# Transposes of two attention stages split off, and products of the conditioning vectors moved ahead of them

## What is computed

```
sh1, sc1, g1, sh2, sc2, g2 = split(silu(c) @ w_ada[l] + b_ada[l], 6)     # conditioning vectors, also for c_ctx
h  = rmsnorm(x) * (1 + sc1) + sh1                                        # 4 tiles of 128 tokens
q, k, v = projections of h @ w_in                                        # 8 MLA heads and 4 differential heads
p  = softmax(q k^T * scale)           # MLA head: one map.  differential head: p0 - lam * p1, two maps
o  = p v ;  x = x + g1 * (concat(o, rmsnorm(o_diff)) @ w_out)
h  = rmsnorm(x) * (1 + sc2) + sh2
x  = x + g2 * peer_ffn(h)             # 8 heads x 16 picked experts for each token, rows gathered from HBM
```

## Time and profile before

| | us |
|---|---|
| median of 3 runs | 2626.43 (2625.87 to 2627.11) |
| the profiled execution, its own time | 2625.7 |
| its span in the trace | 2623.7 |
| granted TensorE clock, mean | 0.904 |

### The profile page before, as it was taken

One profiled execution on the slowest core, in us unless ns is written; L12 is line 12 of the kernel. 1 busy time (PEld: TensorE's weight loads), 2 busy tenths in 40 slices (PEclk: granted clock), 3 DMA queues, 4 the chain that ended last, 5 costly groups with the idle time before them and its releaser, 6 DMA issues.

```text
span 2623.7 us, 26515 instructions
## 1 busy us (share of the span) xinstructions
PE 2058.3 (78%) x6888; PEld 1072.0 (41%) x6888; DVE 1854.4 (71%) x4488; ACT 1162.2 (44%) x3122; POOL 969.7 (37%) x916
## 2 busy tenths in 40 slices
PE   5997778777988877888777697779777887667765
PEld 2555444543444444444334244334553444333322
DVE  0147986895567879886979766655597786877776
ACT  2123484344237543853434723432244754433333
POOL 1013344342434333543443444420133343345553
PEclk8998899887989988998888999999988998899889
DMA  9588999997999899999999999995799989999997
GB/s 339 177 296 322 387 381 398 398 394 278 410 397 420 343 406 381 403 390 411 412 414 397 384 418 418 391 396 195 271 411 385 410 341 380 418 390 420 421 422 321
DMA packets 215707, 980.27 MB, mean 374 GB/s; under 512 B 17660, under 2 KB 75544, under 8 KB 117272
## 3 DMA queue, kind: packets, MB, share of 16 engines
q0 software_dynamic: 123648, 855.69, 80.0%
q1 hardware_dynamic: 91928, 123.05, 13.7%
HBM read 977.62 MB, written 1.05 MB: 373 GB/s over the span
## 4 chain that ended last, share of the span: by engine, by line
PE 29%; DVE 24%; DMA 23%; ACT 14%; issue 8%; POOL 1%; SPq 0%; POOLq 0%; DVEq 0%; ACTq 0%
DMA EXPERT<-in_peer_uv,FIX 21%; PE VS L1008 11%; PE PA L863 9%; DVE EXPERT L1636 8%; DVE ACC L1646 3%; DVE SCR L1262 2%; ACT L1209 2%; PE PA L891 2%; ACT L1157 2%; ACT WEI L1211 1%; PE PB L787 1%; PE PB L998 1%; ACT DIAG L1216 1%; ACT SCR L1157 1%; PE VS L816 1%
## 5 line engine op out<-in xcount | busy, mean ns | idle before, releaser
L1008 PE MATMUL VS<-EXPERT,DIAG 128*128 128x512 f32 x2304 | 1177.6, 652 | 271.4 <-ACT DIAG L1216 266.7
L695 POOL DMA_INDIRECT EXPERT<-in_peer_uv,FIX x768 | 893.7, 1164 | 1110.9 <-PE VS L1008 736.3
L1636 DVE CUSTOM_DVE_ANT_0 EXPERT<-EXPERT,H 128x1024 f32<-128x1024 f32 x768 | 924.9, 1223 | 341.7 <-DMA EXPERT<-in_peer_uv,FIX 330.6
L1008 PEld LDWEIGHTS VS<-EXPERT,DIAG 128*128 128x128 f32 x2304 | 456.9, 209 | 847.7 <-issue 479.3
L1209 ACT ACTIVATE GEL<-DOT 128x1 f32<-128x1 f32 x768 | 155.0, 202 | 1038.6 <-DVE DOT L1636 999.5
L863 PE MATMUL PA<-WT,HT 128*128 128x512 f32 (+2 forms) x720 | 296.0, 557 | 14.6 <-issue 4.3
L1646 DVE SCALAR_TENSOR_TENSOR ACC<-EXPERT,WEI,ACC 128x1024 f32<-128x1024 f32 x192 | 246.1, 1282 | 40.3 <-ACT WEI L1211 40.2
L1216 ACT ACTIVATE DIAG<-IDN,WEI 128x128 f32<-128x128 f32 x576 | 231.3, 402 | 45.9 <-PE VS L1008 27.8
L998 PE MATMUL PB<-HT,WT 128*128 128x128 f32 (+1 forms) x1472 | 210.1, 303 | 38.7 <-issue 37.4
L1211 ACT ACTIVATE WEI<-GEL,GATE 128x1 f32<-128x1 f32 x768 | 226.3, 295 | 24.9
L998 PEld LDWEIGHTS PB<-HT,WT 128*128 128x128 f32 x1472 | 202.7, 214 | 64.1 <-issue 61.0
(11 more groups left out here) (149 smaller groups left out, 1736.1 us busy)
## 6 DMA issues: line engine op xcount, KB each, us to landing
EXPERT<-in_w_ada POOLq DMA_DIRECT2D x48, 1024.0 KB, 12.1
WT<-in_peer_wq SPq DMA_DIRECT2D x92, 512.0 KB
WT<-in_w_in SPq DMA_DIRECT2D x48, 512.0 KB
WT<-in_w_out SPq DMA_DIRECT2D x48, 512.0 KB
EXPERT<-in_peer_uv,FIX POOLq DMA_INDIRECT x768
WT<-in_w_in SPq DMA_DIRECT2D x16, 384.0 KB
WT<-in_w_in SPq DMA_DIRECT2D x16, 288.0 KB
WT<-in_mla_wq_up SPq DMA_DIRECT2D x4, 512.0 KB
```

Source lines behind the costliest of these rows:

```text
L695: pool.indirect_dma_start(out=EXPERT[:, j, :], out_offset=None, in_=a["peer_uv"], in_offset=bass.IndirectOffsetOnAxis(ap=FIX[:, par, j:j + ...
L1008: ins = nc.tensor.matmul(VSUM[n][:, :], DIAG[:, i, :], EXPERT[:, j, D + n * W:D + (n + 1) * W], start=first, stop=last_one)
L1636: nc.vector.tensor_tensor_reduce(out=EXPERT[:, j, 0:D], in0=EXPERT[:, j, 0:D], in1=H2[:, b % HB, :], scale=1.0, scalar=0.0, op0=ALU.mult, ...
```

## The change

Three things:

1. For the two attentions named above, T(i-1) is taken out of the TensorE part of `attn` i and becomes a stage `flip` i behind it. `flip` exists on TensorE alone. All other attentions keep the order of before.
2. In the first, `mingle` now puts the product that followed `attn` i between `attn` i and `flip` i, that is ahead of T(i-1). An `adat` is held back until after the `flip`. So products stand ahead of T(0), T(1), T(3), T(4), T(5), T(6), T(8), T(9), T(10), T(11); before, each stood right behind that same T.
3. In the pause, of the vectors of layer 1: the third product of g1 moves behind `norm`, its fourth behind the `kv` projection; its `adat` from ahead of `root` to behind the key transposes. The second product of sh2 moves from before `root` to ahead of T(8), the third and fourth to ahead of T(9) and T(10), the first of sc2 to ahead of T(11), the second right behind T(11). `adat` of sh2 and of sc2 move from the tail of the attention to behind the `w_out` products, `mod` behind `stat`. Of g2 one product stays ahead of `norm`, three go behind the first pick; so does its `adat`. `gates` (a DVE operation of this attention) moves from behind step 9 to behind step 3.

```diff
+def apart(l, g, t):
+    return (l, g, t) in ((0, CTX, 0), (1, LAT, 0))
+
+def flips(i):
+    return 1 <= i <= MH + DH

 def attention(l, g, t):
-    out = [("attn", l, g, t, i) for i in range(-1, MH + DH + 2)]
+    out = []
+    for i in range(-1, MH + DH + 2):
+        out += [("attn", l, g, t, i)] + ([("flip", l, g, t, i)] if apart(l, g, t) and flips(i) else [])
...
         to = done * len(second) // total
+        if n + 1 < len(first) and first[n + 1][0] == "flip":
+            to = min([to] + [i for i in range(at, len(second)) if second[i][0] == "adat"])
...
-    attend, leave, first = gates_early(attention(0, CTX, 0), 4), outward(0, CTX, (0,)), pick_apart(0, CTX)[0]
+    attend, leave, first = gates_early(attention(0, CTX, 0), 5), outward(0, CTX, (0,)), pick_apart(0, CTX)[0]
...
-    keys, attend, leave = front(1, LAT, (1,), queries=False), gates_early(attention(1, LAT, 0), MH + 3), outward(1, LAT, (0,))
+    keys, attend, leave = front(1, LAT, (1,), queries=False), gates_early(attention(1, LAT, 0), MH), outward(1, LAT, (0,))
...
-    plan += keys[:1] + g1 + [("adae", 1, 2)] + keys[1:at] + sh2[:2] + [("adat", 1, 2)] + keys[at:]
-    at = attend.index(("attn", 1, LAT, 0, MH + DH - 2)) + 1
-    plan += attend[:at] + [sh2[2], attend[at], sh2[3], ("adae", 1, 3), attend[at + 1], sc2[0], attend[at + 2], ("adat", 1, 3)]
-    plan += attend[at + 3:-4] + sc2[1:2] + attend[-4:-2] + sc2[2:] + [("adae", 1, 4)] + attend[-2:] + [("adat", 1, 4), ("mod", 1, 2)]
-    plan += leave[:-2] + products(1, 5) + [("adae", 1, 5), leave[-2], ("adat", 1, 5)] + first[:4] + leave[-1:]
+    plan += keys[:1] + g1[:2] + keys[1:2] + g1[2:3] + keys[2:at] + g1[3:] + [("adae", 1, 2)] + sh2[:1] + keys[at:] + [("adat", 1, 2)]
+    fill = {9: sh2[1:2], 10: sh2[2:3], 11: sh2[3:] + [("adae", 1, 3)], 12: sc2[:1]}
+    for s in attend[:-4]:
+        if s == ("attn", 1, LAT, 0, MH + DH + 1):
+            plan += sc2[1:2]
+        plan.append(s)
+        if s[0] == "attn":
+            plan += fill.get(s[4], [])
+    plan += attend[-4:-2] + sc2[2:] + attend[-2:] + [("adae", 1, 4)]
+    plan += leave[:-3] + [("adat", 1, 3), ("adat", 1, 4)] + leave[-3:-2] + [("mod", 1, 2)] + g2[:1] + leave[-2:-1]
+    plan += first[:3] + g2[1:] + [("adae", 1, 5), first[3], ("adat", 1, 5)] + leave[-1:]
...
-                if 1 <= i <= MH + DH:
...
+                if flips(i) and not apart(l, g, t):
+                    flip(stage)
+
+            def flip(stage):
+                _, l, g, t, i = stage
+                keys = 2 * P if g == CTX else 4 * P
+                h = i - 1
+                bank = fill_a()
...
+                turned.append(ra.n)
```

More of the change, by code:

```diff
@@ L202, in mingle @@
     return out + second[at:]
-COST = {"stat": (45, 0), "norm": (50, 0), "in": (0, 20), "turn": (0, 10), "root": (5, 5), "up": (0, 25), "attn": (35, 0),
+COST = {"stat": (45, 0), "norm": (50, 0), "in": (0, 20), "turn": (0, 10), "root": (5, 5), "up": (0, 25), "attn": (35, 0), "flip": (0, 0),
         "hnorm": (20, 0), "heads": (20, 0), "gates": (10, 0), "rows": (10, 0), "out": (0, 22), "back": (20, 0), "pick": (45, 0), "more": (40, 0), "also": (45, 0), "then": (40, 0),
@@ L319, in make_plan @@
     plan.insert(plan.index(("close", 3)), ("wide", 1))
[L320 removed]
+    keys, attend, leave = front(1, LAT, (1,), queries=False), gates_early(attention(1, LAT, 0), MH), outward(1, LAT, (0,))
     first, picks = pick_apart(1, LAT)
[L322 removed]
+    g1, sh2, sc2 = (products(1, n) for n in (2, 3, 4))
+    g2 = products(1, 5)
     at = keys.index(("root", 1, LAT, "kv", (1,)))
[L324 to L328 removed]
+    plan += keys[:1] + g1[:2] + keys[1:2] + g1[2:3] + keys[2:at] + g1[3:] + [("adae", 1, 2)] + sh2[:1] + keys[at:] + [("adat", 1, 2)]
[9 more added lines that the diff above has]
+    plan += first[:3] + g2[1:] + [("adae", 1, 5), first[3], ("adat", 1, 5)] + leave[-1:]
     rest = first[4:] + front(1, LAT, (1,), keys=False) + attention(1, LAT, 1) + outward(1, LAT, (1,)) + picks[:6]
@@ L941, in attn @@
                     last.then_inc(filled_a, 1)
-                if 1 <= i <= MH + DH:
[L943 to L952, removed]
+                if flips(i) and not apart(l, g, t):
[5 more added lines that the diff above has]
+                bank = fill_a()
+                if h < MH:
+                    pe.wait_ge(exp_ready, tick.so_far("heads") + 1)
+                else:
+                    pe.wait_ge(mixed_ready, tick("mixed"))
+                tick("heads")
+                turn_tiles(bank, [PR[:, h % 2, 0, k * P:(k + 1) * P] for k in range(keys // P)], P)\
+                    .then_inc(filled_a, 1)
+                turned.append(ra.n)
             turned = []
@@ L1032, in _ @@
             do = {"consts": consts, "tables": tables, "ada": ada, "adat": adat, "norm": norm, "back": back, "in": product, "out": product,
-                  "up": up, "turn": turn, "attn": attn, "heads": heads, "rows": rows, "pick": pick_, "more": more, "slots": slots,
-                  "close": close}
+                  "up": up, "turn": turn, "attn": attn, "flip": flip, "heads": heads, "rows": rows, "pick": pick_, "more": more,
+                  "slots": slots, "close": close}
             for stage in PLAN:
```

## The result

The changed kernel takes 2651.93 us, median of 5 runs (2643.53 to 2653.70), beside 2626.43 for the kernel before, in 5 runs of the same series. The ratio is 1.008 with an interval of 1.0056 to 1.0105: slower, and outside the range of the prediction. The profiled execution took 2653.7 us, span 2651.7, mean granted clock 0.899.

A forecast was written before the change was run, and what follows sets the result against it. TensorE's own chain was taken to bound the two stretches without an expert stream. Start +5.3 and pause -2.0 (keys -2.2, attention +2.4, tail -2.2) on 2625.7, median 0.7 above, gave 2629.7 us, range 2623 to 2634.5.

The forecast's parts named there:

- The sum for the order: Context attention at the start: moving products ahead of T costs +5.3 us in all, bounds +3.5 and +8.
- step 7: Context attention: the product ahead of T lengthens a loop through the exponential that had hidden it, +1.0 us.
- steps 3 and 4: Context attention: +0.47 us, because only S stays between T and PV to cover DVE's copy.
- The same wait stays, so I leave the fall where it is.: Context attention, step 8: TensorE's 2.34 us wait stays, so half clock stays at 160.4 to 167.2, no added cost.
- rival C: Context attention: new idle times make the clock fall earlier or longer, 3.1 us more, total 2632.8; chance 0.15.
- Pause, keys: Pause: reciprocal sooner -1.0, clock holding at the key product -1.7, `adat` ahead of the first scores +0.5; sum -2.2 us.
- Rival B: Pause: the clock falls all the same, with little TensorE work before the key product; 1.7 us back, 2631.4; chance 0.2.
- Pause, attention: Pause's attention: products ahead of T(8) and T(9) cost +1.0 each, the next two +0.2 each; sum +2.4 us.
- Pause, tail: End of the pause's attention: `w_out` comes 6.2 us behind the last PV instead of 8.5, -2.2 us.
- g2 behind the pick: Pause: three g2 products behind the first pick are covered by DVE's top-16, costing nothing; otherwise POOL loses up to 1 us.

The follow-up runs named there:

- filler3: Kernel before with the new order in the context attention only, plus unused matmuls: five in step 8's wait, one in each of steps 2 to 9; 2641.63 us, 1.0041.
- after_again: The changed kernel measured once more in another series, against the kernel before; 2645.75 us against 2631.46, ratio 1.0052.
- filler: Changed kernel plus one unused 96x256 matmul ahead of PV in steps 2 to 9 of the context attention; 2642.75 us, 1.006 of the kernel before.
- pause_only: Kernel before with only the pause changed, the context attention as before; 2633.67 us, ratio 1.002.
- mixed: Kernel before with new places of g1 and the two tail `adat`s, two g2 products behind the first pick, both attentions in old order; 2628.49 us, 1.0005.
- warm: Kernel before plus eight unused matmuls in the long wait of step 8 of the context attention; 2632.02 us, ratio 0.9998.
- keys_only: Kernel before with only the new places of g1's products and its `adat` in the pause; 2632.80 us, ratio 0.9997.
- g2_only: Kernel before with only g2 moved: three products, `adae` and `adat` behind the first pick; 2637.23 us, ratio 1.0017.

## Why the prediction was wrong, step by step

**The sum for the order held.** At full clock, with the fillers' overruns taken off, the new order costs 41.1 - 35.75 = **5.4; forecast 5.3**. By steps, from T to T at full clock and with the same overruns taken off, new less old:

| steps | forecast | measured |
|---|---|---|
| 1, and the end | +0.2 | +0.3 |
| 2 | +0.47 | +0.38 |
| 3 and 4 | +0.47 | +1.1 |
| 5 and 6 | +0.7 | +0.8 |
| 7 and 8 | +1.0 | +0.2 |
| 9 | +1.3 | +1.0 |
| 10 to 12 | +1.15 | +1.55 |

The total is right partly by luck. Too high was step 7: the product fits into the loop through the exponential, because T(5) to T(6), which now holds it, is 2.60 where it was 2.44, and T(6) to T(7) stays at 2.86 where it was 2.80. Missed were steps 3 and 4, with the `adat` that waits for ACT's copy (0.48 in `filler3` too), a second work that hangs on the same late exponential.

**The step that failed** is "The same wait stays, so I leave the fall where it is." The wait did stay, 2.34 us to the digit. The fall did not. The old order has 3.4 or 6.8 us at half clock in the five profiles without fillers, the new one 23.9 in three and 17.1 in the fourth. Set against the full-clock lengths: the new order loses 50.42 - 41.1 = 9.3 us by the clock, the old one 38.35 - 35.75 = 2.6, so **6.7 us** of the 12.1 are the clock and 5.4 the order. In `after_again` it is 47.07 - 41.1 - 2.6 = 3.4.

That is rival C, by its own test: the granted clock left 1.00 at 150, long before T(7) at 163.8. It was back at 153 and fell once more, for 20 us, behind the long wait, so both things happened that C named. Its mechanism was right and its price, 3.1, was less than half of the 6.7 of the first profile (and about the 3.4 of the second), because I let the fall last no longer than once more the old one. What I had against it, that the pause's attention holds 1.00 with waits of the same size, was weak evidence: the same attention, with the same instructions, ran 0, 10.2 and 17.1 us at half clock in later profiles (41.46, 44.58 and 46.99 us long). The trace agrees in part with the section of the Trainium skill that the prediction named for C (TensorE: Matmul & The Clock Gate, "A second HAM failure mode: psum-queue depth-cycling"). The short waits go with a clock that falls twice and fillers in them and in the long wait with 1.00; but the second time the clock stays at 0.50 for 20 us (14 in `after_again`) instead of going back and forth.

**Pause, keys.** The reciprocal came sooner as forecast (-1.0), and the clock held at the key product in six of seven profiles (-1.7). What I did not ask is what the third and fourth product of g1 had covered in their old place: TensorE's wait for `norm`. Rival B said that the clock would fall all the same; it fell at another place in five of the seven, and in the changed kernel for so long that this gave back more than had been won (+0.3 instead of -2.2).

**Pause, attention.** From S(0) to the last PV it took 38.6 us before and 41.5 in `filler`, at full clock: +2.9 (forecast +2.4). In the changed kernel, its repeat and `pause_only` it was 43.0, +4.4, with 3.4 us at half clock, a fall that the sum did not have.

**Pause, tail.** Last PV to `w_out` went from 8.46 to 6.08, -2.4 (forecast -2.2). This term held.

**g2 behind the pick.** Costed at nothing, or 1 on POOL if the cover fails. The cover did fail, 0.73. From `w_out` to the first gather pass 35.1 us in the six profiles that keep the old places of g2 and of the `adat`s, and 35.7 in `after_again`, `pause_only` and `mixed`. The weight pieces of the next query, which I had not followed past the moved products, add some 1.7 behind the gather.

**Sum.** Order 5.4 and clock 3.4 make 8.8 in the start of `after_again`; its pause, from the first spread gate to the first gather, is 2.8 longer (126.1 against 123.3), and the first slots behind it add 1.7: 13.3, beside +13.7 by its ratio. The first profile has 5.4 + 6.7 in the start and 4.0 in the pause, 17.8 with the 1.7, beside +21 by the first ratio. So a pause forecast at -2.0 came out at +2.8 to +4.0; most of the difference is half clock in its keys and its attention. What the first profile has above that (+28, 11 of it in the streams, where the change touches nothing) stays open. The stream of layer 0 alone lasts from 1524.2 to 1535.3 us in the thirteen profiles, whatever the order of the start.

No variant beat both kernels: `warm`, `mixed`, `keys_only` and `g2_only` can't be told from the kernel before.

## What to carry to other kernels

Find out on which side of an instruction the wait lies before moving work: here it lay between the transpose and the product that needs it, and the moved work had been what filled it. Work that fills a wait may also be what holds the clock, so removing it can cost twice; list the new short waits in a row and price them at half clock for the whole of the stretch, not for one fall. When fillers are used to measure an order at full clock, take off what they outlast their waits by: here the two errors, 0.85 in one run and 1.81 in the other, were as large as a term of the sum. And when work moves behind a release (an index list, a weight slot), follow both queues that hang on it.

## What was not expected of the hardware

With waits of only 0.6 us, one in each step, a clock that had fallen stayed at 0.50 for 14 to 20 us in four profiles. With the short waits of steps 2 to 9 filled it was 10.2 (one profile), and with the long wait filled as well it never fell (two profiles). What an additional microsecond at half clock costs is about 0.5 us in these steps ((50.42 - 47.07) / (23.9 - 17.1)). And the same instructions ran with quite different clocks from one execution to the next: the unchanged attention of the pause had 0, 10.2 or 17.1 us at half speed, worth 5.5 us, which alone is the size of what a measurement of this kernel can tell.
